# A decoder trunk on one core: the spread of H at a change of phase is split around the first pair of gathers

## What is computed

```python
def peer_ffn(h, w_q, sub_keys, u_tab, v_tab):
    q = (h @ w_q).reshape(bsz, seq, PEER_HEADS, 2, PEER_HALF)
    s = einsum('blhpe,hpne->blhpn', q, sub_keys)
    s_top, i_top = top_k(s, 16)                      # of 128 keys, for both halves
    cand = s_top[..., 0, :, None] + s_top[..., 1, None, :]
    best, pos = top_k(cand, 16)                      # of 256 sums
    idx = expert numbers of those 16
    gate = softmax(best)
    # per token: 8 heads x 16 experts = 128 rows of u_tab and v_tab
    act = einsum('cd,ckd->ck', h, u_tab[idx])
    return einsum('ck,ckd->cd', gate * gelu(act), v_tab[idx])

for i in range(2):
    h = rms_norm(x, norm_mix[i]);  x = x + mixer_i(h)
    h = rms_norm(x, norm_ffn[i]);  x = x + peer_ffn(h, ...)
return rms_norm(x, norm_final)
```

## Time and profile before

| | |
|---|---|
| time, median of 3 runs | 1818.57 us (1815.49 to 1819.64) |
| the profiled execution | 1814.31 us, its span 1812.5 us |
| PE busy | 1286.4 us, 71% of the span |
| DVE busy | 1157.7 us, 64% |
| POOL busy | 637.8 us, 35% |
| ACT busy | 554.8 us, 31% |
| moved by DMA | 685.26 MB, 378 GB/s over the span; 72.5% of the DMA engines' time is the gathers |

### The profile page before, as it was taken

How to read it: one execution, slowest core, us unless ns; L and a number is a source line. 1 busy time by engine, 2 the same in 40 slices (tenths; PEclk the granted TensorE clock), 3 DMA queues, 4 the chain that set the end, 5 groups by cost and what they waited for, 6 DMA issues and landing times.

```text
span 1812.5 us, 17056 instructions
## 1 busy us (share of the span) xinstructions
PE 1286.4 (71%) x5712; PEld 538.8 (30%) x5712; DVE 1157.7 (64%) x2784; ACT 554.8 (31%) x1472; POOL 637.8 (35%) x559
## 2 busy tenths in 40 slices
PE   3676455558776897898869689789877874555554
PEld 2364011112351233333327123353353630100000
DVE  8955989885467757535646684744453667777554
ACT  6422321111223316313512231551271132122111
POOL 5102334443323324324422332332332334454442
PEclk9897668678897999998889689999998968677877
DMA  7039889999999999999999899999999979999997
GB/s 310 1 121 402 330 317 392 386 392 409 425 421 365 373 425 420 423 424 423 420 424 423 348 371 425 421 366 418 413 391 413 421 309 413 415 415 404 423 421 307
DMA packets 88649, 685.26 MB, mean 378 GB/s; under 512 B 12144, under 2 KB 12272, under 8 KB 14320
## 3 DMA queue, kind: packets, MB, share of 16 engines
q0 software_dynamic: 73728, 536.90, 72.5%
q1 hardware_dynamic: 14832, 147.26, 19.5%
HBM read 683.08 MB, written 1.05 MB: 377 GB/s over the span
## 4 chain that ended last, share of the span: by engine, by line
PE 33%; DMA 31%; DVE 22%; ACT 7%; issue 4%; POOL 2%; SPq 0%; POOLq 0%; ACTq 0%; DVEq 0%
DMA ringmem<-experts,lay 19%; PE ps L436 11%; PE ps L406 11%; DVE ringmem L1060 7%; DMA wt<-w_qkv 7%; PE ps L446 4%; POOL ringmem L1028 2%; DMA wt<-w_q 2%; ACT lay L762 2%; DMA wt<-w_o 2%; PE ps L421 2%; ACT S L713 1%; PE ps L625 1%; PE ps L600 1%; PE ps L512 1%
## 5 line engine op out<-in xcount | busy, mean ns | idle before, releaser
L1028 POOL DMA_INDIRECT ringmem<-experts,lay x512 | 602.3, 1176 | 1089.1 <-PE ps L406 951.3
L406 PE MATMUL ps<-ringmem,S 128*32 128x512 f32 x2048 | 618.8, 765 | 412.7 <-ACT S L713 412.6
L1060 DVE CUSTOM_DVE_ANT_0 ringmem<-ringmem,Hrep 128x1024 f32<-128x1024 f32 x512 | 614.9, 1222 | 221.4 <-DMA ringmem<-experts,lay 215.4
L406 PEld LDWEIGHTS ps<-ringmem,S 128*32 128x32 f32 x2048 | 113.0, 127 | 830.9 <-ACT S L713 585.0
L708 ACT ACTIVATE gelus<-dots 128x2 f32<-128x2 f32 x256 | 52.2, 204 | 840.8 <-DVE dots L1060 840.3
L436 PE MATMUL ps<-wt,hT 128*128 128x512 f32 x576 | 256.2, 598 | 15.4 <-DMA wt<-w_qkv 15.3
L436 PEld LDWEIGHTS ps<-wt,hT 128*128 128x128 f32 x576 | 106.5, 190 | 165.2 <-issue 159.2
L713 ACT ACTIVATE S<-S,gelus 128x32 f32<-128x32 f32 x512 | 136.7, 314 | 24.0 <-ACT gelus L708 0.4
L446 PE MATMUL ps<-hT,wt 128*128 128x128 f32 x1024 | 119.8, 279 | 2.8 <-DMA wt<-w_q 1.7
L446 PEld LDWEIGHTS ps<-hT,wt 128*128 128x128 f32 x1024 | 117.1, 194 | 14.2 <-DMA wt<-w_q 6.1
L1357 DVE TENSOR_TENSOR area<-ps,con 128x512 f32<-128x512 f32 x24 | 16.6, 692 | 150.5 <-PE ps L436 146.3
(11 more groups left out here) (187 smaller groups left out, 1124.2 us busy)
## 6 DMA issues: line engine op xcount, KB each, us to landing
wt<-w_qkv SPq DMA_DIRECT2D x36, 2048.0 KB, 11.6
wt<-w_q SPq DMA_DIRECT2D x16, 2048.0 KB, 11.9
wt<-w_glu SPq DMA_DIRECT2D x5, 2048.0 KB, 11.9
ringmem<-experts,lay POOLq DMA_INDIRECT x512, 12.3
wt<-w_o SPq DMA_DIRECT2D x4, 2048.0 KB, 14.1
ringmem<-w_glu SPq DMA_DIRECT2D x3, 2048.0 KB, 17.0
gain<-gains SPq DMA_DIRECT2D x9, 512.0 KB, 12.2
area<-keys SPq DMA_DIRECT2D x4, 1024.0 KB, 9.7
```

Of the source, the lines that this page charges most:

```text
L406: last = pe.matmul(ps[TG * t:TG * (t + 1), half, :], S[:, u % 2, i, :], ring[:, (2 * u + i) % RING, D + half * 512:D + (half + 1) * 512], ...
L1028: pool.indirect_dma_start(ring[:, s % RING, :], None, experts[phase // NC], bass.IndirectOffsetOnAxis(ap=rows[:, phase % NC, j, n:n + 1], ...
L1060: last = v.tensor_tensor_reduce(ring[:, i, 0:D], ring[:, i, 0:D], Hrep[:, j, :], 1.0, 0.0, ALU.mult, ALU.add, dots[:, b, second:second + 1])
```

## The change

Four edits.

1. `spread_h` on PE and ACT, for phases 1 to 3: after 4 of the 8 matmuls (and copies) stands pair 1. `Hrep` for j = 0 and 1 is all that pair 1 needs.
2. The root is taken by ACT behind pair 2 and no longer in the middle of the spread; DVE does pair 2 too before it waits for the root and writes H. In phase 3 no root stands there before or after.
3. `PARTS_AT`: the 12 parts move from pairs 1, 2, 3, 4, 5, 6, 8, 9, 11, 12, 15, 16 to pairs 2, 3, 4, 5, 6, 8, 9, 11, 12, 14, 15, 16. ACT has an explicit `g.at` for the pair of the first quarter's gates, which goes from 4 to 5.
4. PE's four waits before it writes into the score banks are on `best_ready` and not on `idx_ready`.

```diff
-        PARTS_AT = (1, 2, 3, 4, 5, 6, 8, 9, 11, 12, 15, 16)
+        PARTS_AT = (2, 3, 4, 5, 6, 8, 9, 11, 12, 14, 15, 16)
...
                 for u in range(2 * QUAD):
                     j, half = divmod(u, 2)
                     rows_j = slice(TG * j, TG * (j + 1))
+                    if phase and u == QUAD:
+                        g.at(phase, 1)
...
-                    pe.wait_ge(idx_ready, QUARTERS)
+                    pe.wait_ge(best_ready, QUARTERS)
...
-                            pe.wait_ge(idx_ready, QUARTERS * (c + 1) + 2)
+                            pe.wait_ge(best_ready, QUARTERS * (c + 1) + 2)
...
-                            pe.wait_ge(idx_ready, QUARTERS * (c + 2))
+                            pe.wait_ge(best_ready, QUARTERS * (c + 2))
...
                 for u in range(2 * QUAD):
                     j, half = divmod(u, 2)
+                    if phase and u == QUAD:
+                        g.at(phase, 1)
                     act.wait_ge(h_spread, 2 * QUAD * phase + u + 1)
                     act.copy(Hrep[:, j, half * 512:(half + 1) * 512],
                              ps[:, src[u % len(src)], :]).then_inc(hrep_ready, 1)
-                    if e is not None and u == 3:
-                        root(e)
+                if e is not None:
+                    g.at(phase, 2)
+                    root(e)
...
                 copy_turn(hT, turned, e + 1, hT_ready)
+                g.at(gphase, PARTS_AT[3])
                 gate_quarter(c + 1, 1)
...
-                norm(gphase, 0, c, norm_event(1, c, 0), normed, h_spread, 2 * QUAD * (2 + c))
+                norm(gphase, 1, c, norm_event(1, c, 0), normed, h_spread, 2 * QUAD * (2 + c))
```

## The result

| | before | changed |
|---|---|---|
| median | 1818.98 us (8 runs) | 1833.82 us (8 runs) |
| lowest to highest | 1815.49 to 1825.03 | 1828.63 to 1840.17 |
| profiled execution, its span | 1814.31, 1812.5 | 1835.09, 1833.3 |

The ratio is 1.0083, with a 95% interval of 1.0064 to 1.0102: the change costs 15 us; 14 were forecast.

A forecast was written before the change was run, and what follows sets the result against it. Between changes of phase the DMA engines bound the kernel. The three changes of phase summed to 11.3 us (2.4 GHz) or 18.5 us (1.2 GHz), taken as 14: a median of 1832.5 us, range 1815.5 to 1841.

The forecast's parts named there:

- Pair 1 within the spread: Phase 0 to 1: pair 1 on PE at 562.9, not 569.25, taking 3.4 us; two gathers issued 6.4 us earlier.
- The second half of the spread: Phase 0 to 1: starts at 566.2, not 560.0; last copy at 571.3 (2.4 GHz) or 573.2 (1.2 GHz).
- The root behind pair 2, and H: Phase 0 to 1: 5.3 us in a row behind the last copy; H at 576.6 or 578.5, 8.7 or 10.6 us later.
- From H to projection 0: DVE, ACT, PE chain: projection 0 at H + 31.9 (was H + 33.5), so 608.5 or 610.4 instead of 601.4.
- DMA time: Cost of the late projection 0: 5.8 or 7.7 us at phase 0 to 1, 5.9 or 7.8 at phase 1 to 2.
- Phase 2 to 3: No root or projection there: idle 9.8 us against 6.8, +3.0 us, or -0.4 at 2.4 GHz.
- PARTS_AT and best_ready: Moved selection parts and PE's changed waits before the score banks: each claimed to change nothing.
- The table load in H's way: Between pair 2 and the root: priced at 1.28 us; the skill's 2.66 us would make H another 1.4 us later.
- The signs that were named: DMA share 570 to 576 rises; H 576 to 579, 1032 to 1035; projection 0 near 609, 1065; idle in two or three pieces.
- The clock: PE in the spread: by the skill's rule the new 2 us pause leaves every second half at 1.2 GHz, 18.5 us.
- Rival A: Faster: the chain from H does not hold projection 0, DVE has place; some 8 us gained, for 1810; 13 in 100.

The follow-up runs named there:

- E7: The changed kernel with PARTS_AT = 5 to 16, so the selection parts stand beside the projections; ratio to before 0.9952.
- E4: The kernel before with edit 4 alone: PE's waits before it writes into the score banks are on best_ready, not idx_ready; ratio to before 0.9994.
- E9: The kernel before with the spread split around pair 1 in phase 3 only; ratio to before 1.0000.
- E3: The kernel before with edit 3 alone: the moved PARTS_AT and the explicit g.at ahead of the first gates; ratio to before 0.9995.
- E1: The kernel before with edit 1 alone: pair 1 in the middle of the spread, the root still behind the fourth copy; ratio to before 1.0104, +19 us.
- E8: The kernel before with pair 1 mid-spread, the root behind pair 1's scaling, and PARTS_AT = 5 to 16; ratio to before 0.9971, -5 us.
- E6: The kernel before with late parts only: PARTS_AT = 5 to 16, one part a pair, beside the projections; ratio to before 0.9930, -12.7 us.
- E10: The changed kernel with PARTS_AT = 5 to 16 and its spread whole in phase 3; ratio to before 0.9924, -14 us.

## Why the prediction was right

Right in sign, size and mechanism. That 14 came so near to 15 is in part luck: it was taken between 11.3 us (second halves of the spread at 2.4 GHz) and 18.5 (all at 1.2), and of the three second halves of after the first ran at 2.4 GHz and the other two at 1.2. With the prediction's own prices for that mix the sum is 5.8 + 7.8 + 3.0 = 16.6 us; the stretches of the two profiles give 5.2 + 7.5 for the first two changes, and dry time 0.1 for the third. By its own steps:

- **Pair 1 within the spread.** Pair 1 on PE at 562.9: it was at 562.93. Its first gather at 566.5: 566.84. It took 3.63 us and not 3.4. But the gain was over-sized: the queue was to hold work until about 571, and from 566 to 570 the share is already 0.72 (above), before pair 1's gathers flow. Some 1.2 us of the work before had there is a 0.52 MB transfer of `gain` (an estimate, at 425 GB/s), which SP issues once H is written: at 567.88 in before, at 576.28 in after.
- **The second half of the spread.** Last copy 571.3 with the clock at 2.4 GHz: it ended at 571.1.
- **The root behind pair 2, and H.** H at 576.6: 576.25. At the second change 8.8 or 10.7 us were forecast for H's delay, and it was 11.5, counted from the first copy (1041.07 less 1019.11, against 1023.62 less 1013.13). There the clock had fallen within the first half already (granted 0.50 from 1021 on), and the second half took 6.5 us on PE instead of 4.0 (the last two rows are the halves at the third change):

```profile
1017.90 4.51 PE L423 MATMUL ps<-H,con 32*128 32x512 f32 x8
...
1028.77 6.52 PE L423 MATMUL ps<-H,con 32*128 32x512 f32 x8
...
1488.94 4.52 PE L423 MATMUL ps<-H,con 32*128 32x512 f32 x8
...
1499.83 6.52 PE L423 MATMUL ps<-H,con 32*128 32x512 f32 x8
```

- **From H to projection 0.** H + 31.9 gives 608.2 with the measured H; it was 608.18. This is the best-founded step, and E7 confirms it by removal: with no part behind H the way from H to projection 0 is 19.1 us, and the delay of projection 0 shrinks from 6.1 and 9.4 us to 0.6 and 1.2.
- **DMA time.** 5.8 us at the first change: 50.7 + 410.9 less 44.6 + 411.8 is 5.2. At the second 5.9 or 7.8: 54.2 + 416.9 less 44.8 + 418.8 is 7.5. Nothing behind gave it back, as forecast. Against the same stretches of E4 and E9 the differences are smaller (4.4 and 2.5 at the first, 6.2 and 3.0 at the second), so the agreement to about half a microsecond is better than single profiles can show.
- **Phase 2 to 3.** -0.4 or +3.0: E9 gives 0.0, with 3.3 us to either side; in its profile the second half took 4.40 us, most of it at 2.4 GHz, the case of -0.4. The changed kernel's own profile has 343.1 us for its last stretch against 335.8, but its dry time there is 6.9 us against 6.8, so I do not read that as the split's. Its second half there took 6.52 us, at 1.2 GHz, for which +3.0 was the forecast; that was too much. Of the 2.0 + 7.8 us that the forecast has, the 2.0 ahead of pair 1's gathers are not there: the share from 1498 to 1504 is 0.97.
- **PARTS_AT and best_ready.** Nothing for each: E3 and E4.
- **The table load in H's way** was priced at the row's 1.28 us. In after it starts at 573.24 and the root at 574.53 (rows above); reciprocal and H follow at 574.77 and 574.97. The further 1.4 us for a drain, which the Trainium skill has in ScalarE: Activation LUTs, section What ACT_TABLE_LOAD costs, are not to be seen between load and root.
- **The signs that were named.** The share from 570 to 576 rose from 0.34 to 0.69, and H and projection 0 came as forecast at the first change. At the second, put on the time scale of before, they are at 1035.1 and 1067.3, a little later than 1032 to 1035 and 1065. The dry time is in four pieces and not two or three. Pair 2's gathers at the last change are issued at 1499.5 on that scale, so later than 1497, which goes with the 1.2 GHz there.
- **The clock.** Its paragraph reads the new pause of some 2 us as leaving every second half at 1.2 GHz. That reading went further than the rows could carry it, and the runs do not bear it out as a rule: behind the same pause of 2.8 us the second half of the first change ran at 2.4 GHz (3.98 us), those of the other two at 1.2 (6.52 us each).

What the prediction did not see: that edit 1 by itself, with the root left in the spread, carries the whole loss, and that edit 2 on top of it adds nothing that can be seen (E1 against the changed kernel). In my sum both were terms of one chain to H, and I had not asked what each would do without the other. For E1, I forecast +8 to +13 us and got 19. H's delay was 5.7 and 8.4 us where 5.5 to 7.5 were expected, and all of it reached projection 0 (6.3 and 9.0 us), since in E1 pair 2 is not yet done when H is written; the size of the loss was missed.

Rival A (faster, since DVE's chain does not hold projection 0) fell: the chain does hold it.

**Open:** why late parts gain 12.7 us with only 2.4 us less of dry time at the two changes; why E8 is 5 to 7 us above E6 when its projections start only 2.2 and 0.1 us later; and how much of E7's 4 to 6 us is phase 3, which E9 measures as nothing and E10 suggests to be something (E10 has it whole and is at E6's level, from another session).

## What to carry to other kernels

When an ordered engine program is bound by transfers, ask of each early release what comes later for it, and what long work is queued behind that: here two gathers came 7 us earlier, those of the third pair 3 us later, and four selection steps with them. A step that delays the head of such a queue costs little once the queue is moved to where its engine has room; moving the twelve parts was worth 13 us, and no order of the spread was seen to gain anything. And test each edit of a bundle alone: two of the four did nothing, one cost 19 us and one 5, and the four together 15.

## What the hardware showed that I had not expected

PE's clock within a dense run of matmuls on 32 rows fell at different points of the same program: the first eight records of the spread (two to a matmul) took 4.20 us at the first change of after, 4.51 at the second and 4.52 at the third, and the second eight 3.98, 6.52 and 6.52, behind a pair 1 of 3.63 us each time. In the first case the granted clock rose to 2.4 GHz within half a microsecond of pair 1's end (1.00 from 567 on), in the others it stayed at 1.2 GHz through the second half (0.50). E7 has the second halves of its first two changes at 2.4 GHz and that of the third at 1.2. I found nothing in the program that differs ahead of them, so a term with this clock in it should be forecast at both levels, as a range.
